# A two-FFN decoder layer on eight cores: smaller first column blocks, first loads in pieces and in another order, identity matmuls in the first gaps, the last tile in pieces

## The reference

```python
x = x + 0.5 * swiglu(rmsnorm(x, norm_ffn1), ffn1_gate, ffn1_up, ffn1_down)
h = rmsnorm(x, norm_mix)
proj = h @ w_in                       # [B | C | u | p], 4 x 512 columns
y_conv = B * conv3_causal(C * u)      # 3 taps per channel
y_pool = scale * (trailing means of p over 2, 4, 8, 16 tokens, minus the token) @ pool_w
x = x + concat(y_conv, y_pool) @ w_out
x = x + 0.5 * swiglu(rmsnorm(x, norm_ffn2), ffn2_gate, ffn2_up, ffn2_down)
y = rmsnorm(x, norm_final)
# swiglu(h) = (silu(h @ w_gate) * (h @ w_up)) @ w_down, hidden width 2816 = 22 chunks of 128
```

## Time and profile before

| | us |
|---|---|
| median of 3 runs | 1221.24 |
| lowest run | 1220.32 |
| the profiled execution's own time | 1222.25 |
| its span on the slowest core (core 6), first to last instruction | 1220.7 |
| spans of the other cores | 1212.7 to 1219.8 |
| TensorE busy (share of the span) | 1173.4 (96%) |
| VectorE busy | 605.4 (50%) |
| ScalarE busy | 274.7 (22%) |
| GpSimd busy | 164.3 (13%) |

### The profile page before, as it was taken

The page is one execution under the profiler, slowest core; times in us unless marked ns, Lnnn a source line. Parts: engine busy times, 40 slices in busy tenths (PEclk is TensorE's granted clock), DMA queues, the critical chain, the costliest instruction groups (busy, mean ns, idle before and its releaser), DMA issues.

```text
span 1220.7 us, 19560 instructions; the slowest of 8 cores (1212.7 to 1220.7 us)
## 1 busy us (share of the span) xinstructions
PE 1173.4 (96%) x6740; PEld 626.0 (51%) x6740; DVE 605.4 (50%) x948; ACT 274.7 (22%) x649; POOL 164.3 (13%) x283
## 2 busy tenths in 40 slices
PE   6499999999999999989999989999999999999996
PEld 5264544445445444467677744454454454454544
DVE  3364434334344354787677653443343344444478
ACT  3331111111111112345454531011111111111134
POOL 3130000000000001254424330000000000000022
PEclk9799999999999999999999999999999999999999
DMA  9957700700500507395010198033042040050024
GB/s 197 270 96 108 101 3 1 104 1 1 78 1 6 73 1 113 61 137 81 19 36 19 28 148 127 4 49 57 1 69 36 1 64 15 1 79 1 1 113 182
DMA packets 73249, 75.69 MB, mean 62 GB/s; under 512 B 47680, under 2 KB 47808, under 8 KB 73152
## 3 DMA queue, kind: packets, MB, share of 16 engines
q0 software_dynamic: 20880, 41.03, 23.1%
q1 hardware_dynamic: 52272, 33.41, 11.0%
HBM read 94.15 MB, written 10.03 MB: 85 GB/s over the span
## 4 chain that ended last, share of the span: by engine, by line
PE 91%; DMA 6%; DVE 1%; issue 1%; ACT 1%; SPq 1%; POOL 0%; POOLq 0%; DVEq 0%; ACTq 0%
PE ps L504 52%; PE ps L536 25%; PE ps L603 7%; PE ps L784 4%; PE ps L626 3%; DMA ring<-ffn_down 2%; DMA gbc<-norm_mix 1%; DMA ring<-w_in 1%; DMA ring<-ffn_up 1%; DMA gbc<-norm_ffn 1%; SPq L365 0%; ACT junk L386 0%; PE ps L761 0%; DVE xres L543 0%; PE ps L423 0%
## 5 line engine op out<-in xcount | busy, mean ns | idle before, releaser
L504 PE MATMUL ps<-hT,ring 128*128 128x512 bf16 (+2 forms) x3696 | 687.4, 341 | 16.1 <-DVE hT L433 11.3
L504 PEld LDWEIGHTS ps<-hT,ring 128*128 128x128 bf16 x3696 | 337.9, 99 | 347.8 <-issue 19.6
L516 DVE TENSOR_TENSOR scr<-scr,ps 128x512 bf16<-128x512 f32 (+2 forms) x231 | 135.2, 586 | 463.6 <-PE ps L504 457.2
L536 PE MATMUL ps<-ring,scr 128*128 128x512 bf16 x1496 | 357.7, 380 | 6.3 <-DMA ring<-ffn_down 4.9
L543 DVE SCALAR_TENSOR_TENSOR xres<-ps,xres 128x512 f32<-128x512 f32 x408 | 276.3, 690 | 53.2 <-PE ps L536 47.0
L514 ACT ACTIVATE scr<-ps 128x512 f32<-128x512 f32 (+2 forms) x231 | 118.8, 515 | 777.7 <-PE ps L504 768.4
L536 PEld LDWEIGHTS ps<-ring,scr 128*128 128x128 bf16 x1496 | 144.5, 98 | 172.6 <-issue 11.0
L603 PE MATMUL ps<-hT,ring 128*128 128x256 bf16 (+1 forms) x864 | 95.4, 267 | 3.2 <-DVE vext L730 3.2
L386 ACT ACTIVATE junk<-xres 128x1024 bf16<-128x1024 f32 x68 | 71.8, 1056 | 79.5 <-DVE xres L543 52.6
L603 PEld LDWEIGHTS ps<-hT,ring 128*128 128x128 bf16 x864 | 80.7, 98 | 14.7 <-issue 3.7
L331 POOL DMA_DIRECT2D ring<-ffn_gate x11 | 8.4, 761 | 555.7 <-PE ps L504 543.5
(11 more groups left out here) (61 smaller groups left out, 287.8 us busy)
## 6 DMA issues: line engine op xcount, KB each, us to landing
xres<-xp SPq DMA_DIRECT2D x16, 512.0 KB, 9.4
ring<-ffn_down POOLq DMA_DIRECT2D x8, 1024.0 KB, 14.2
yp<-xres SPq DMA_DIRECT2D x16, 512.0 KB, 2.6
ring<-ffn_gate POOLq DMA_DIRECT2D x7, 1024.0 KB, 11.5
ring<-ffn_up POOLq DMA_DIRECT2D x7, 1024.0 KB, 16.6
ring<-w_in POOLq DMA_DIRECT2D x4, 1024.0 KB, 13.6
ring<-ffn_gate POOLq DMA_DIRECT2D x4, 768.0 KB, 9.2
ring<-ffn_up POOLq DMA_DIRECT2D x4, 768.0 KB, 13.0
```

Source lines behind the costliest of these rows:

```text
L504: ins = e.matmul(ps[bank][:, 0:N], lhsT=ring_gu(slot)[:, jj, kc, :], rhs=hT[:, kc, tok0:tok0 + N], start=(kc == 0), stop=(kc == KC - 1))
L516: P.op("dve", lambda e: e.tensor_tensor(out=aT[:, buf, jj, off:off + N], in0=sg[:, sk, 0:N], in1=ps[ub][:, 0:N], op=ALU.mult), reads=[("sg ...
L536: ins = e.matmul(ps[db][:, 0:512], lhsT=aT[:, buf, jj, ti * 128:(ti + 1) * 128], rhs=ring_dn(ds)[:, jj, dh * 512:(dh + 1) * 512], start=(j ...
```

## The change

1. `BLOCKS` differ by FFN: FFN1 3, 4, 4, 4, 4, 3 chunks; FFN2 2, 4, 4, 4, 4, 4.
2. First loads: gate and up of three chunks and down of three chunks, each its own 0.5 MB transfer; x 4, x 5 when gate chunk 1 has landed, x 6 to 16 when down chunk 0 has landed. The channel constants, `norm_mix`, `pexts`, `vexts`, `poolw` move behind the landing of block 1's down (`load_late`). Slots are tracked by chunk.
3. `PE_TILES` is 10. The 24 identity matmuls become 18 operations of 8, which the scheduler may place where TensorE would idle.
4. The mixer runs its groups in the order 0 to 6, 8, 7; in the last one `mix_pool_win` comes first, and gate and up of FFN2's block 0 (two chunks each) share slot 3, down goes to slot 0.
5. The last tile (`finish_last`): down in pieces of 512, 256 and 256 columns, squares by piece, product with the gain ahead of the power, the last scaling split over VectorE (640 columns) and ScalarE (384), and two output transfers.
6. The scheduler models DMAs as queues that share a rate. This changes the order on every engine.

```diff
-BLOCKS = [[0, 1, 2, 3], [4, 5, 6, 7], [8, 9, 10, 11], [12, 13, 14, 15], [16, 17, 18], [19, 20, 21]]
+BLOCKS = {1: [[0, 1, 2], [3, 4, 5, 6], ..., [15, 16, 17, 18], [19, 20, 21]],
+          2: [[0, 1], [2, 3, 4, 5], ..., [14, 15, 16, 17], [18, 19, 20, 21]]}
-PE_TILES = 8
+NFILL = 18
+PE_TILES = 10
...
-        for _ in range(24):
+        for _ in range(8):
             ins = e.matmul(ps[5][:, 0:128], lhsT=idb[:, :], rhs=idb[:, :], start=True, stop=True)
...
-    load_first_jj(0, after=(xload[1],))
+    load_first("g", 0, after=(xload[1],))
+    load_first("u", 0)
     for tt in range(4):
         norm(tt, 0, pe=True)
-    for jj in range(1, 4):
-        load_first_jj(jj)
-    load_x(4, after=(unit_ops[("jj", 1, 2)],))
-    for tt in range(5, 8):
+    for jj in range(1, 3):
+        load_first("g", jj)
+        load_first("u", jj)
+    load_x(4, after=(first_ops[("g", 1)],))
+    load_x(5)
+    for jj in range(3):
+        load_first("d", jj)
+    load_x(6, after=(first_ops[("d", 0)],))
+    for tt in range(7, NT):
         load_x(tt)
-    load_unit(ffn1_down, 0, 4, slot=2)
-    load_x(8, after=(unit_ops[2],))
-    for tt in range(9, NT):
-        load_x(tt)
-    P.op("sp", lambda e: e.dma_start(out=cw[:, :], in_=chan[:, :]), writes=[("cw",)], dma=True, c=420, nbytes=8192, chain=True)
-    load_gbc(1, norm_mix)
...
+    for i in range(NFILL):
+        P.op("pe", warm_up, reads=[("idb",)], writes=[("ps", 5)], c=8 * (107 if i < 7 else 56))
+    def load_late(gate):
...
+        load_gbc(1, norm_mix)
...
+    MIX_ORDER = [0, 1, 2, 3, 4, 5, 6, 8, 7]
...
+        if final:
+            mix_pool_win(g)
+            load_ffn_part(2, 0, "g", 3, 0)
+            load_ffn_part(2, 0, "u", 3, 2)
...
+    load_ffn_part(2, 0, "d", 0)
...
+    def finish_last(f, b, grp, buf):
+        pieces = ((0, 512, 4), (512, 256, 5), (768, 256, 6))
...
+            load_late(load_ffn_block(1, 1, slots1(1), after=(last_t[0],)))
...
+            load_ffn_block(2, 1, slots2(1), after=(last_t[0],))
```

More of the change, by code:

```diff
@@ L115, in schedule, with release, move @@
         free = {e: 0.0 for e in self.ENGS}
-        lines = {"sp": 0.0, "pool": 0.0}
+        queue = {"sp": [], "pool": [], "act": []}
+        clock = 0.0
+        landing = []
         out = {e: [] for e in self.ENGS}
         todo = len(self.order)
+        def release(o, us, w):
+            for u in us:
+                left[u] -= 1
+                at[u] = max(at.get(u, 0.0), w + (self.LAT[u.eng] if (u.eng != o.eng or o.dma) else 30))
+                if not left[u]:
+                    ready[u.eng].append(u)
+        def move(limit):
+            nonlocal clock
+            while True:
+                heads = [q[0] for q in queue.values() if q and q[0][1] <= clock]
+                stop = min([limit] + [q[0][1] for q in queue.values() if q and q[0][1] > clock])
+                if heads:
+                    rate = 0.29 / len(heads)
+                    stop = min(stop, clock + min(h[2] for h in heads) / rate / 1000)
+                    for h in heads:
+                        h[2] -= (stop - clock) * rate * 1000
+                clock = max(clock, stop)
+                for q in queue.values():
+                    if q and q[0] in heads and q[0][2] < 1:
+                        landing.append((clock + 1500, q.pop(0)[0]))
+                if clock >= limit:
+                    return
         while todo:
@@ L125, in schedule @@
                         pick = ((t, o.gidx), o)
-            (t, _), o = pick
+            t = pick[0][0] if pick else clock + 500
+            move(max(clock, min(t, clock + 200)))
+            done = [z for z in landing if z[0] <= clock + 1500]
+            if done:
+                for z in done:
+                    landing.remove(z)
+                    z[1].done = z[0]
+                    release(z[1], users[z[1]], z[0])
+                continue
+            if clock < t:
+                continue
+            o = pick[1]
             e = o.eng
@@ L130, in schedule @@
             free[e] = t + o.cost
+            o.done = free[e]
+            todo -= 1
+            release(o, issued[o], free[e] - 30)
             if o.dma:
[L132 to L135, removed]
-            else:
[L137 to L149, removed]
+                queue[e].append([o, free[e] + 700, float(o.nbytes)])
+            else:
+                release(o, users[o], free[e])
         self.byeng = out
+        move(clock + 1e6)
+        for z in landing:
+            z[1].done = z[0]
         return max(o.done for o in self.order)
@@ L352, in load_first_jj, with load_unit @@
[L352 to L359, removed]
+    def load_unit(W, c0, nb, slot, off=0, after=()):
+        src = W[c0:c0 + nb].rearrange("j p f -> p j f")
+        dst = ring[:, slot, off * 1024:(off + nb) * 1024].rearrange("p (j f) -> p j f", j=nb)
+        return P.op("pool", lambda e: e.dma_start(out=dst, in_=src), dma=True,
+                    writes=[("ring", slot, off + jj) for jj in range(nb)],
+                    after=after, c=900, nbytes=nb * 128 * 4096, chain=True)
@@ L577, in run_ffn @@
                 block_start(b)
-            if prev is not None and prev[0] == len(BLOCKS) - 1:
+            if prev is not None and prev[0] == 5:
                 post(prev[1])
             prev = (b, g, idx % 2)
+        if last is not None:
+            last(f, *prev)
+            return
         for emit in ffn_D_ops(f, *prev):
```

200 lines of the change are left out of this document (116 added, 84 removed).

## The result

The changed kernel takes 1213.01 us (median of 5 runs, 1212.55 to 1213.41), the kernel before 1220.78 (median of 4): ratio 0.9936, 95% interval 0.9921 to 0.9952. So it is faster, by 0.64% or 7.8 us, where I forecast 23 us (1198.0, range 1189 to 1211). In some executions the cores of one die or of both have a lower granted clock and the time is 2 to 19% longer; such runs are left out of every median here, which leaves 3 runs or more of each kernel and one of experiment 11.

A forecast was written before the change was run, and what follows sets the result against it. TensorE's matmuls set the 1220.7 us span; idle and half-clock time could be won. Gains 16.5 + 4.8 + 2.0 = 23.3, taken as 23.0, from 1222.25 gave 1199.2, and 1198 as median; range 1189 to 1211.

The forecast's parts named there:

- new waits of more than 5 us between 60 and 1180: Sign on the timeline, in us, that would show the forecast wrong; the other was group 2 beginning after 63.
- Start, 16.5: Start of FFN1 up to group 2: time beside its own matmuls falls from 44.1 to 27.6 us, gain 16.5.
- the stall for x 4's square: FFN1's start: ScalarE has x 4's square ahead of a silu, so TensorE stops from about 24.0 to 28.0, 4.0 us.
- the landing of x 4: FFN1's start: loads move 4.9 us earlier, gate chunk 1 landing at about 17.3 and x 4 at 26.2.
- What is late next: Rest of FFN1's start: block 1 in time; DMA transposes from tile 10 counted as costing nothing, 3 us at most.
- Mixer to FFN2, 4.8: Handover from mixer to FFN2: 6.5 us of waits and half clock go, new waits come, net gain 4.8 us.
- the wait ahead of the last matmul, 0.7: End of FFN2: TensorE's wait for the last 6 down matmuls shrinks from 1.21 to about 0.5 us, gain 0.7.
- the wait for window sums (1.0): Mixer to FFN2: second pool product waits for GpSimd's sums behind two weight issues, 0 to 2.4 us, taken as 1.0.
- End, 1.3: Behind the last matmul: the chain to the span's end takes 6.9 us against 8.2, gain 1.3.
- New waits in its place: Rival: x 4 later, down lower, another clock fall, transposes of tiles 10 and 11 held; 8 us worse, 1206; chance 0.2.
- the slower case: Rival at the start: clock stays at 1.2 GHz from 15 to 56 us, about 1224 us; chance 0.03.
- The rule on pieces: Start's 0.5 MB loads: skill says batch DMAs to ≥1 MiB; by it group 2 would start some 3 us later.

The follow-up runs named there:

- experiment 11: Changed kernel with its planner counting a DMA transpose as landed 6.0 us after its transfer instead of 1.5: 1211.96 us in a single run.
- experiment 3: Changed kernel with the two 2 MB loads of `w_out` issued only once tile 15's transpose has landed: 1201.50 us.
- experiment 9: Kernel of experiment 1 with the scaling of the last norm's weights also moved later on VectorE, behind the last product of mixer group 1: 1201.08 us, ratio 0.9821.
- experiment 4: Changed kernel with the squares of x 4 and x 5 on ScalarE placed behind the first group's fourth silu: 1213.36 us.
- experiment 5: Kernel of experiment 3 with x 4's load released by the first gate column's first piece instead of its second: 1202.89 us.
- experiment 6: Kernel of experiment 3 without the 24 identity matmuls ahead of the first gate matmul: 1201.57 us.
- experiment 7: Kernel of experiment 3 with the last tile finished as in the kernel before, without pieces: 1201.24 us.
- experiment 1: Changed kernel with tile 16's `hp` write moved 23 rows later on VectorE, behind the fourth conv product of mixer group 0: 1206.14 us.
- experiment 12: Kernel of experiment 3 with 24 identity matmuls in place of 144: 1202.10 us, from runs of 1200.74, 1202.10 and 1207.03.

## Why the prediction was wrong

*The step that failed* is none of its terms: it is the stretch between FFN1 and the mixer, of which the prediction says nothing and so counts as unchanged. It named the sign to look for ("new waits of more than 5 us between 60 and 1180") but did not look for its cause. It cost 11.7 us: tile 16's `hp` had been put ahead of the mixer's products and waited 11.22 us for a held transpose. Without that the forecast would have been near, though still some 3 us low: experiments 3 and 9 take 1201.5 and 1201.1 us, with 1198.0 predicted. The terms that the sum does have come to 14.2 + 6.9 + 0.1 = 21.2 instead of 23.3. What was to be seen was there: the change rewrites the scheduler (its item 6), and I compared orders only at the start. Of held transposes I had a row, and asked of it only whether the tiles come too late, not which buffer stays taken and what VectorE has behind the row that wants it.

*Start, 16.5: was 14.2.* The identity matmuls end at 11.0 (11.4 predicted), the stall for x 4's square is 4.80 (4.0), and down waits for nothing, as said. The mis-sized term is the landing of x 4: gate chunk 1 landed at 18.8, not 17.3, and x 4 at 28.38, not 26.2. So TensorE goes on at 30.02 instead of 28.0, which is 2.0 of the 2.3 us by which group 2 is late. The first gate is late too, at 17.38 and not 15.3: the first transpose waits until 12.86, and the last 24 identity matmuls take 2.77 us behind it, at half clock. But that falls into the time in which TensorE would wait for x 4 anyway: core 6 has its first gate at 17.22 and group 2 at 55.23, core 4 has them at 14.56 and 56.42. Experiments 4 and 5 show that the terms are not to be added: the square and x 4's late landing were each taken away, and another wait filled the place; nor did the time change without the 24 matmuls (experiment 6).

*"What is late next"*: the transposes from tile 10 on cost nothing at the start, as counted, and block 1 was in time.

*Mixer to FFN2, 4.8, and the wait ahead of the last matmul, 0.7: 5.5, measured 6.9.* The first gate has no wait, as said; the wait for window sums (1.0) and that of the sample group (0.7) did not come, so all 6.5 were won. The last wait fell from 1.21 to 0.83, not to 0.5; by experiment 7 what is left of it comes with the pieces.

*End, 1.3: was 0.1.* The order of rows was right, the chain not: the three squares run one behind the other on ScalarE until 1205.7, then come GpSimd's last two additions and its power until 1207.1, and the last scaling begins at 1207.30, 1.65 us after the end of tile 15's. I had counted the matmul's addition and product, but neither that chain of squares nor GpSimd's steps. Experiment 7 confirms that the time gains nothing.

*Rivals.* "New waits in its place" had the right kind of loss, but too small (8 us, 1206) and in the wrong place; its own mechanism, x 4, down and tiles 10 and 11, would have cost at the start and at most 2.3 us were lost there. The clock did not stay low at the start (0.91 and 0.83 in the first two stretches of 20 us, 1.00 in the third), so the slower case fell.

*The rule on pieces.* In the first and second 20 us the changed kernel moved 195 and 261 GB/s, the kernel before, with its 2 MB transfer in the second, 203 and 193. So these rows show no loss by pieces of 0.5 MB, but they don't test it, since the kernel before had fewer transfers in flight in the second 20 us. By the rule of the Trainium skill (DMA: Bandwidth & Descriptors, Bandwidth) I had estimated 3 us more. x 4 was 2.2 us late and group 2 was 2.3, while TensorE waited for no down weights; no run here with larger pieces says whether that is the rule's doing.

## What to carry to other kernels

A change of a scheduler must be read on every engine over the whole program: one row of `hp` ahead of the wrong neighbours cost 11.7 us. Moving it gave 6.9 back, and the rest came only when the row that its move had upset was moved too. When an instruction moves, look for what waits for its buffer on other queues: the load that overwrites its operand moved with it, and the row that wants this load did not. Of a wait for a buffer ask how long the reader may be held at its worst, and put nothing urgent behind it.

## What the runs showed of the hardware

A DMA transpose of one tile, SBUF to SBUF, took 3.0 to 3.3 us in most cases when no weights were in flight (median 3.1, up to 5.3 in the profiles here). With only the 2 MB load of `p` in flight it took up to 6.7 us in experiment 3 and 8.2 in experiment 5. Issued just behind the first half of `w_out`, with the second half following, it took 16.5 and 16.9 us (experiments 12 and 7). With three loads in flight it took 19 to 22 us, and the issue of the second of two such transposes then blocked SyncE's queue for 12.9 to 14.8 us. The Trainium skill says on ordering of such transfers that "A transpose next to ordinary DMAs needs nothing" (DMA: Bandwidth & Descriptors, Rules for kernel authors). It speaks of correct data, and the traces say nothing against that; on time they show the hold above.

Two transfers of the same kind and size differed sixfold by what was in flight from another queue. I had expected a slower rate; what the rows show looks like a hold: in the changed kernel the two transposes, issued at 516.99 and 518.65, landed at 537.03 and 537.93, the first as the second half of `w_out` was in (537.02). In experiments 1, 7, 9 and 12 the held transpose landed within 0.3 us of that load too. What in the DMA queues makes it wait, no run here shows.
